# Second block: GLA score pieces as three fp32r products, and an earlier order for the gates and a later one for the MLA latents

## The chip, the cores and the metric

The kernel runs on one core of one Trainium2 chip. Times are device microseconds from launch to end. Three runs of the kernel before gave 2714.05, 2717.61 and 2721.09 us; their median, 2717.61, is what a forecast is compared with.

## The reference, cut to what matters

The program is two transformer-like blocks in a row, each with two layers, on 256 tokens of width 1024. All arithmetic is fp32. The change touches the second block's mixer alone, which runs once per layer:

```python
zin = h @ w_in
(cq, ckv, kpe, sg_uv, gq, gk, gv, g_lr, g_og, dq, dk, dv, da, db, dz, gates) = split(zin)
o_a = mla_branch(cq, ckv, kpe, ...)          # latents -> norm -> w_uq, w_ukv -> rope -> attention
o_b = spatial_gating_branch(sg_uv, ...)
o_c = gla_branch(gq, gk, gv, g_lr, g_og, ...)
o_d = deltanet_branch(dq, dk, dv, da, db, dz, ...)
```

The gated linear attention (GLA) computes, for 4 heads with keys of 32:

```python
log_a  = log_sigmoid(gate_lr @ w_gate + b_gate) / 16     # low-rank gates, per head and key element
cum    = cumsum(log_a)
scores = einsum('bhik,bhjk,bhijk->bhij', q, k, exp(cum_i - cum_j)) for i >= j
o      = scores @ v   (and the carried state; then norm and output gate)
```

## The kernel before, in words

**Matrix work.** The kernel keeps fp32 accuracy in its projections by splitting each operand into a high part, rounded to fp32r, and a low part, what is left, also held as fp32r. A product is then three fp32r products: low with high, high with low, high with high. ScalarE (ACT) makes the high part of the weights (`hi`), VectorE (DVE) the low part by a subtraction (`lo`). Smaller products inside the branches are plain fp32 matmuls. In the trace a plain fp32 matmul leaves two weight loads and two matmul records, an fp32r one leaves one of each, and so does a transpose.

**Parts.** The weights of one pass of the second block come in 84 parts of 128x2048 elements through a ring of three buffers. SyncE (SP) starts the load of part h once the low part of h-3 is made. Parts 0 and 1 are the MLA latents (`cq_fill`), part 2 a few narrow columns, among them the low-rank gates, parts 3 to 11 the other projections, parts 12 to 31 the gates and the branch products. `in_fill(h)` runs the 48 products of a part in two halves, m = 0 and m = 1, each of 8 steps k of three products with 256 columns streamed, which I call wide products.

**The order is written out by hand.** TensorE (PE) calls `between(h, m, k)` after each step, `mid(h)` between the halves and `after(h)` at the end of part h; there the small products of the branches are put. ACT and DVE run loops over i, where `hi(i + 2)` and `lo(i + 1)` alternate with what belongs to the branches. Semaphores hold the rest: `pe.wait_ge(sem, n)` stands in PE's queue, and everything behind it waits too.

**GLA scores.** The lower triangle of the 256x256 scores is put together from 9 levels j: one for the block of the second half of the tokens against the first (j = 0), seven for halves within ever smaller squares, and one (j = 4) with the raw q and k for the diagonal. For each level q and k are scaled by exp of a difference of cumulated logs (`level_diffs`, `level_exps`, `level_inputs`), four levels at a time: qeA, keA and then qeB, keB. A level has 8 pieces (4 heads, 2 blocks of 128 tokens; level 0 has 4), each a product over the 32 rows of a head, 128 columns loaded and 128 streamed. `gla_piece(j, p)` runs one piece per step of parts 13 to 17. DVE takes each level out of PSUM by a masked copy (`scores`), and two levels' PSUM banks alternate, so level j waits for the copy of j-2. `gla_out` multiplies the scores with v.

**What else the change moves.** `c_turn` transposes the MLA latents, `mla_up` projects them up, `rope_turn` does the rotation's half turn, `few_turn` does gate_lr @ w_gate and the transposes of the narrow columns, `softplus_1` to `_3` make the log gates, `cumulate` and `cumulated` their cumulative sums, `squared_norms` the deltanet's key norms, `decay_rows`, `kv_turn`, `lower_rows` and `key_products` belong to the deltanet's triangular system. The rows of `mem`, needed for cross attention, are loaded to `xm`, which shares its place with `probs`.

Of the kernel before, what the change touches and what calls it, by code (L numbers as in the profile page):

```python
# [7 lines left out]
F32 = mybir.dt.float32  # L8
# [8 lines left out]
P = 128  # L17
SEQ = 256
# [1286 lines left out]
def second_block(nc, ps, x, con, bfc, a):  # L1305
    with ExitStack() as ctx:
# [40 lines left out]
        qeB, keB = at("qeB", [P, 4, SEQ], offset=base), at("keB", [P, 4, SEQ], offset=base + 4096)  # L1347
        gates = at("gates", [P, 2, KD, SEQ], offset=base + 8192)
# [14 lines left out]
        qeA, keA = at("qeA", [P, 4, SEQ], offset=base), at("keA", [P, 4, SEQ], offset=base + 4096)  # L1363
        l2s, l2r = at("l2s", [P, 4, SEQ], offset=base + 8192), at("l2r", [P, 4, SEQ], offset=base + 12288)
# [10 lines left out]

        probs = at("probs", [P, 8, SEQ])
        xm = probs[:, :, :].rearrange("p (t a) b -> p t (a b)", t=NT)
# [5 lines left out]
        spb = at("spb", [P, 5, 264], offset=base)  # L1383


        base = place[0]
        dnp = at("dnp", [P, 6, SEQ + 4])
        rv, kd = at("rv", [P, NT, W2], offset=base), at("kd", [P, W2], offset=base + 2048)
# [38 lines left out]
        cum_ps, df_ok, le_ok, lev_ok = sem("cum_ps"), sem("df_ok"), sem("le_ok"), sem("lev_ok")  # L1427
        sa_zero, gp_ps, sa_ok, go_ps, go_ok, sil_ok, gn_ok = (
# [86 lines left out]
        def level(j):  # L1515


            if j == 4:
                return gqk[:, 0, :], gqk[:, 1, :]
            n = j if j < 4 else j - 1  # L1520
            return (qeA[:, n, :], keA[:, n, :]) if n < 4 else (qeB[:, n - 4, :], keB[:, n - 4, :])
# [60 lines left out]
        with nc.Fori(0, DEPTH) as l:  # L1582
            with nc.Block() as block:

                @block.sync
                def _(sp_):
# [35 lines left out]
                    for h, (_, _, source) in enumerate(parts):  # L1622
# [12 lines left out]
                        if h == 17:  # L1635

                            sp_.wait_ge(pt_ps, 1)
# [4 lines left out]
                def _(pe):  # L1642
# [135 lines left out]
                    def few_turn():  # L1778
                        pe.wait_ge(*freed[unit["in", FEW2]])
                        for t in range(NT):  # L1780
                            T.matmul(ps[:, 3, t * P:(t + 1) * P], fewS[:, t * P:(t + 1) * P], wg[:, :],
                                     start=True, stop=True)
                        for t in range(NT):
                            mm = T.transpose(ps[:, 3, SEQ + t * P:SEQ + (t + 1) * P], fewS[:, t * P:(t + 1) * P], ident)
# [1251 lines left out]
```

## Time and profile before

| | |
|---|---|
| median of three runs | 2717.61 us (2714.05 to 2721.09) |
| the profiled execution | 2721.69 us, its span 2719.9 us, mean granted TensorE clock 0.935 |
| PE busy | 2527.3 us, 93% of the span |
| DVE busy, ACT busy | 1424.9 us (52%), 1092.8 us (40%) |
| DMA | 370.35 MB, mean 136 GB/s |

The first block takes the time to about 1261 us, then come the second block's two passes, from 1291 us and from 2000 us. The profile's line PEclk gives the TensorE clock granted in each of 40 slices of 68 us, in tenths of full speed. The clock has two levels, 2.4 GHz (1.00) and 1.2 GHz (0.50). "PE" rows are matmuls, whose ends are modelled, "PEld" rows are weight loads. A timeline row gives the start, the length from the first start to the last end, and how many records are merged in it; x2 is one plain fp32 piece. For how long PE is held, the distance from start to start tells more than the lengths, since records overlap.

### The profile page before, as it was taken

To read this page: it belongs to the slowest core of one execution; us is meant where nothing else is said; L and a number is where in the kernel's file an instruction comes from. 1 tells how busy PE (TensorE), PEld (TensorE's weight loads), DVE (VectorE), ACT (ScalarE), POOL (GpSimd) and SP (SyncE) were. 2 spreads that over 40 slices of the span, in tenths; PEclk is the share of its full clock that TensorE was granted. 3 is DMA by queue.
4 is the path that set the end of the run, shared out by engine and by line. 5 is a ranking of instruction groups with operands and counts; after the bars stand their busy time and mean duration, and the time that the engine had idled before them with its cause. 6 is when DMAs were issued, how large, how long until landed. Compare 5 with 4: busy or idle time off the path is not lost. (4 is left out here: it accounts for less than half of the span.)

```text
span 2719.9 us, 40921 instructions
## 1 busy us (share of the span) xinstructions
PE 2527.3 (93%) x17400; PEld 2316.2 (85%) x17400; DVE 1424.9 (52%) x1539; ACT 1092.8 (40%) x1356; POOL 48.4 (2%) x49
## 2 busy tenths in 40 slices
PE   6999998996999998995899999989959999998996
PEld 6988998986988998994787898989859789898985
DVE  6555465455555456453653467445537245754453
ACT  3533544343534444342451324444425213344342
POOL 0000000000000000000000000000000000000000
PEclk9999999998999999997895899999979669999998
DMA  6423455544533354551641234445444213354552
GB/s 200 152 83 113 133 187 167 180 180 116 181 94 94 122 189 155 186 187 55 184 131 31 78 99 150 155 143 183 170 133 128 71 47 94 109 171 155 163 194 85
DMA packets 300003, 370.35 MB, mean 136 GB/s; under 512 B 25006, under 2 KB 267300, under 8 KB 299812
## 3 DMA queue, kind: packets, MB, share of 16 engines
q1 hardware_dynamic: 299812, 367.62, 42.8%
q8 instruction: 142, 2.33, 0.4%
q14 instruction: 49, 0.40, 0.0%
HBM read 366.55 MB, written 1.05 MB: 135 GB/s over the span
## 5 line engine op out<-in xcount | busy, mean ns | idle before, releaser
L398 PE MATMUL ps<-a_nhi,a_wlo 128*128 128x256 f32 x1792 | 524.8, 293 | 12.0 <-DVE a_nlo L951 10.4
L398 PE MATMUL ps<-a_nlo,a_whi 128*128 128x256 f32 x1792 | 507.9, 283 | 0.0
L398 PE MATMUL ps<-a_nhi,a_whi 128*128 128x256 f32 x1792 | 507.6, 283 | 0.0
L921 DVE TENSOR_TENSOR a_wlo<-a_ring,a_whi 128x2048 fp32r<-128x2048 f32 x174 | 395.5, 2285 | 107.9 <-ACT a_whi L705 107.4
L2430 DVE TENSOR_TENSOR b_wlo<-b_ring,b_whi 128x2048 fp32r<-128x2048 f32 (+1 forms) x168 | 379.2, 2261 | 134.9 <-ACT b_whi L2168 134.7
L1669 PE MATMUL ps<-b_nhi,b_wlo 128*128 128x256 f32 x1296 | 414.5, 320 | 19.3 <-ACT b_cqk L2186 11.8
L705 ACT CAST a_whi<-a_ring 128x2048 fp32r<-128x2048 f32 x174 | 331.1, 1905 | 194.9 <-PE ps L398 73.2
L2168 ACT CAST b_whi<-b_ring 128x2048 fp32r<-128x2048 f32 (+1 forms) x168 | 316.1, 1884 | 175.3 <-PE ps L2151 77.4
L1669 PE MATMUL ps<-b_nlo,b_whi 128*128 128x256 f32 x1296 | 386.2, 298 | 0.0
L1669 PE MATMUL ps<-b_nhi,b_whi 128*128 128x256 f32 x1296 | 385.8, 298 | 0.0
L398 PEld LDWEIGHTS ps<-a_nhi,a_wlo 128*128 128x128 f32 x1792 | 345.1, 193 | 18.1 <-DVE a_wlo L921 11.4
L398 PEld LDWEIGHTS ps<-a_nlo,a_whi 128*128 128x128 f32 x1792 | 344.8, 192 | 2.5 <-issue 2.4
L398 PEld LDWEIGHTS ps<-a_nhi,a_whi 128*128 128x128 f32 x1792 | 344.3, 192 | 0.0
L1669 PEld LDWEIGHTS ps<-b_nhi,b_wlo 128*128 128x128 f32 x1296 | 264.1, 204 | 51.1 <-issue 44.9
L1669 PEld LDWEIGHTS ps<-b_nlo,b_whi 128*128 128x128 f32 x1296 | 269.4, 208 | 0.1
L1669 PEld LDWEIGHTS ps<-b_nhi,b_whi 128*128 128x128 f32 x1296 | 268.7, 207 | 0.0
L2196 ACT ACTIVATE b_gates<-ps 128x512 f32<-128x512 f32 x32 | 19.1, 597 | 224.6 <-PE ps L1669 224.6
L2151 PE MATMUL ps<-b_whi,b_hlo 128*128 128x512 f32 x256 | 99.6, 389 | 0.0
L2151 PE MATMUL ps<-b_wlo,b_hhi 128*128 128x512 f32 x256 | 99.6, 389 | 0.0
L2151 PE MATMUL ps<-b_whi,b_hhi 128*128 128x512 f32 x256 | 99.6, 389 | 0.0
L2605 DVE COPY_PREDICATED b_SaT<-b_con,ps 128x1024 f32<-128x1024 uint32 x16 | 21.0, 1311 | 141.3 <-PE ps L1865 141.3
L1242 DVE TENSOR_TENSOR a_gates<-a_ffg,ps 128x512 f32<-128x512 f32 x22 | 15.1, 688 | 142.5 <-PE ps L398 142.5
(531 smaller groups left out, 4604.5 us busy)
## 6 DMA issues: line engine op xcount, KB each, us to landing
a_ring<-in_w_in SPq DMA_DIRECT2D x50, 1024.0 KB, 5.3
b_ring<-in_w_in SPq DMA_DIRECT2D x50, 1024.0 KB, 6.1
a_ring<-in_w_ffn_in SPq DMA_DIRECT2D x44, 1024.0 KB, 5.3
a_ring<-in_w_gate SPq DMA_DIRECT2D x32, 1024.0 KB, 5.3
b_ring<-in_w_up SPq DMA_DIRECT2D x32, 1024.0 KB, 5.6
b_ring<-in_w_down SPq DMA_DIRECT2D x32, 1024.0 KB, 4.9
a_ring<-in_w_ffn_out SPq DMA_DIRECT2D x22, 1024.0 KB, 5.0
a_ring<-in_w_branch SPq DMA_DIRECT2D x16, 1024.0 KB, 5.1
```

What stands on the lines that cost most here:

```text
L398: mm = T.matmul(out, w[:, k, c:c + P], x_[:, k, :], start=k == 0 and n == 0, stop=k == KD - 1 and n == 2)
L705: S.copy(part(whi, h), part(ring, h)).then_inc(hi_ok, 1)
L921: V.tensor_tensor(part(wlo, h), part(ring, h), part(whi, h).bitcast(F32), ALU.subtract).then_inc(lo_ok, 1)
L1242: V.tensor_tensor(hid[:, 2 * c:2 * c + 2, :], ffg[:, c % 2, :].rearrange("p (b c) -> p b c", b=2), ps[:, 4 + c % 2, :].rearrange("p (b c) ...
L1669: mm = T.matmul(out, w[:, k, c:c + P], x_[:, k, :], start=k == 0 and n == 0, stop=k == KD - 1 and n == 2)
L2151: mm = T.matmul(ps[:, 4 + 2 * t + half, :], hidden_of(x_, i)[:, kk, t * P:(t + 1) * P], w[:, kk, half * 512:(half + 1) * 512], start=i + k ...
L2168: A.copy(part(whi, h), part(ring, h)).then_inc(hi_ok, 1)
L2196: ins = A.activation(gates[:, g // 4 % 2, 2 * (g % 4):2 * (g % 4) + 2, :], b.rearrange("p (a b) -> p a b", a=2), gate_func)
L2430: V.tensor_tensor(part(wlo, h), part(ring, h), part(whi, h).bitcast(F32), ALU.subtract).then_inc(lo_ok, 1)
L2605: V.copy_predicated(SaT[:, :, :, :], m, level_out(j)).then_inc(sa_ok, 1)
```

## The change

GLA pieces: the scaled q and k of each group of levels, and the raw ones, get a high part on ACT (`level_hi`, and a copy to qkh) and a low part on DVE (`level_lo`, `raw_lo`). A piece is then three fp32r products. Pieces start half a part later. PE's order of the small products changes: few_turn goes to after part 3 and to PSUM bank 7, c_turn to after part 4, mla_up to after part 5, rope_turn to after part 6, cumulate from after part 9 to after part 7, gla_out into the middle of part 18, kv_turn into the middle of part 19. ACT's and DVE's orders follow, and some waits name other semaphores.

```diff
@@ sync
-                        if h == 17:
-                            sp_.wait_ge(pt_ps, 1)
+                        if h == 21:
+                            sp_.wait_ge(gp_ps, pieces_to(4))
                             sp_.dma_start(xm[:, :, :], a["mem_2"]...).then_inc(mem_in, 16)
@@ tensor: mla_up, few_turn
                         pe.wait_ge(ct_ok, 1)
-                        pe.wait_ge(w_in_, 48)
+                        pe.wait_ge(spv, 1)
...
                         pe.wait_ge(*freed[unit["in", FEW2]])
+                        pe.wait_ge(w_in_, 48)
@@ squared_norms / cumulate / spatial_mix
-                        pe.wait_ge(spv, 1)
+                        pe.wait_ge(eg_in, 1)
-                        pe.wait_ge(l2_rt, 1)
+                        pe.wait_ge(ct_ok, 1)
-                        pe.wait_ge(eg_in, 1)
+                        pe.wait_ge(l2_rt, 1)
@@ gla_piece
                             if j == 0:
-                                pe.wait_ge(lev_ok, 1)
+                                pe.wait_ge(ll_ok, 1)
+                            if j == 4:
+                                pe.wait_ge(qkl_ok, 1)
                             if j == 5:
-                                pe.wait_ge(lev_ok, 2)
+                                pe.wait_ge(ll_ok, 2)
...
-                        q_, k_ = level(j)
+                        q_hi, q_lo, k_hi, k_lo = level(j)
                         r = slice(32 * h, 32 * h + 32)
                         tq_ = 1 if j == 0 else t
-                        T.matmul(level_out(j)[:, h, t, :], k_[r, t * P:(t + 1) * P], q_[r, tq_ * P:(tq_ + 1) * P],
-                                 start=True, stop=True).then_inc(gp_ps, 1)
+                        for n, (k_, q_) in enumerate(((k_lo, q_hi), (k_hi, q_lo), (k_hi, q_hi))):
+                            mm = T.matmul(level_out(j)[:, h, t, :], k_[r, t * P:(t + 1) * P], q_[r, tq_ * P:(tq_ + 1) * P],
+                                          start=n == 0, stop=n == 2)
+                        mm.then_inc(gp_ps, 1)
@@ between / mid / after
-                        if 13 <= h <= 17 and 2 * (h - 13) + m < 9:
-                            gla_piece(2 * (h - 13) + m, k)
+                        if 13 <= h <= 17 and 2 * (h - 13) + m > 0:
+                            gla_piece(2 * (h - 13) + m - 1, k)
...
                         if h == 18:
+                            gla_out()
                             decay_rows()
+                        if h == 19:
+                            kv_turn()
...
                         if h == 3:
+                            few_turn()
+                        if h == 4:
                             c_turn()
-                        if h == 4:
+                        if h == 5:
                             mla_up()
-                            few_turn()
-                        if h == 5:
+                        if h == 6:
                             rope_turn()
+                        if h == 7:
+                            cumulate()
                         if h == 8:
                             squared_norms()
-                        if h == 9:
-                            cumulate()
...
-                        if h == 17:
-                            gla_out()
-                        if h == 18:
-                            kv_turn()
@@ scalar
+                    def level_hi(g, qe_, ke_, qh_, kh_):
+                        act.wait_ge(lev_ok, g + 1)
+                        A.copy(qh_[:, :, :], qe_[:, :, :])
+                        A.copy(kh_[:, :, :], ke_[:, :, :]).then_inc(lh_ok, 1)
...   (latents' eviction from i == 4 to 5, mla_up's from 5 to 6, gate exps 6 to 5, Ln 7 to 6,
...    level_exps(0) 11 to 10, level_exps(1) 14 to 13, squares of mem 20 to 22)
+                        if i == 12:
+                            level_hi(0, qeA, keA, qhA, khA)
+                            A.copy(qkh[:, :, :], gqk[:, :, :]).then_inc(qkh_ok, 1)
...
                         if i == 14:
                             turn_hi(0)
-                            level_exps(1, keB)
+                            act.wait_ge(o_ps, 1)
+                            level_hi(1, qeB, keB, qhB, khB)
@@ vector
+                    def level_lo(g, qe_, ke_, qh_, kh_, ql_, kl_):
+                        dve.wait_ge(lh_ok, g + 1)
+                        V.tensor_tensor(ql_[:, :, :], qe_[:, :, :], qh_[:, :, :].bitcast(F32), ALU.subtract)
+                        V.tensor_tensor(kl_[:, :, :], ke_[:, :, :], kh_[:, :, :].bitcast(F32), ALU.subtract
+                                        ).then_inc(ll_ok, 1)
+
+                    def raw_lo():
+                        dve.wait_ge(qkh_ok, 1)
+                        V.tensor_tensor(qkl[:, :, :], gqk[:, :, :], qkh[:, :, :].bitcast(F32), ALU.subtract
+                                        ).then_inc(qkl_ok, 1)
...   (softplus_1 from i == 5 to 4, _2 from 6 to 5, _3 from 7 to 6; cumulated and level_diffs(0) to 8;
...    level_inputs(0) and level_diffs(1) to 11; level_lo(0) at 12; raw_lo and level_inputs(1) at 13;
...    level_lo(1) at 14; scores(j), turn_lo, gate_gain half a part to one part later;
...    gla_result and lower_rows ahead of lo(20); norm_in(2) from 22 to 23)
```

## Rows read from the trace of the kernel before

**Rows 1.** The page: PE's busy time, and the granted clock in 40 slices.
```profile
PE 2527.3 (93%) x17400; PEld 2316.2 (85%) x17400; DVE 1424.9 (52%) x1539; ACT 1092.8 (40%) x1356; POOL 48.4 (2%) x49
...
PEclk9999999998999999997895899999979669999998
```

**Rows 2.** Windows: length, busy time per engine, granted clock, DMA share, GB/s.
```profile
1318.00:1404.00 86.00, 86.00 (x649) 80.13 (x650) 61.26 (x87) 48.52 (x67) 4.54 (x3) 0.97 0.52 142
1404.40:1417.90 13.50, 13.50 (x76) 10.31 (x75) 4.07 (x8) 4.22 (x6) 0.00 (x0) 1.00 0.41 148
1417.90:1513.40 95.50, 95.39 (x295) 70.64 (x296) 30.85 (x21) 12.76 (x13) 0.00 (x0) 0.50 0.16 44
...
2124.40:2226.80 102.40, 102.29 (x320) 76.18 (x320) 31.81 (x21) 14.12 (x14) 0.00 (x0) 0.50 0.15 41
...
1531.70:1540.60 8.90, 8.90 (x55) 7.04 (x53) 0.00 (x0) 2.33 (x2) 0.00 (x0) 1.00 0.41 118
```

**Rows 3.** Windows, of line L1865 alone: PE and PEld busy, records, clock.
```profile
1404.40:1417.90 13.50, 6.28 (x26) 3.80 (x26) 1.00 0.41 148
1417.90:1513.40 95.50, 43.56 (x110) 27.36 (x110) 0.50 0.16 44
2113.90:2124.40 10.50, 4.75 (x20) 2.91 (x20) 1.00 0.50 189
2124.40:2226.80 102.40, 46.00 (x117) 28.85 (x116) 0.50 0.15 41
```

**Rows 4.** Timelines of PE and PEld, pieces at full clock (start, us).
```profile
1404.41 0.48 PE L1865 MATMUL ps<-b_qeA,b_keA 32*128 32x128 f32 x2
1404.82 0.39 PE L1669 MATMUL ps<-b_nhi,b_wlo 128*128 128x256 f32 x1
...
1405.16 0.28 PE L1669 MATMUL ps<-b_nhi,b_whi 128*128 128x256 f32 x1
1405.37 0.48 PE L1865 MATMUL ps<-b_qeA,b_keA 32*128 32x128 f32 x2
...
1404.82 0.19 PEld L1669 LDWEIGHTS ps<-b_nhi,b_wlo 128*128 128x128 f32 x1
1404.93 0.19 PEld L1669 LDWEIGHTS ps<-b_nlo,b_whi 128*128 128x128 f32 x1
```

**Rows 5.** The same at half clock.
```profile
1426.99 0.79 PE L1865 MATMUL ps<-b_qeA,b_keA 32*128 32x128 f32 x2
1427.71 0.58 PE L1669 MATMUL ps<-b_nhi,b_wlo 128*128 128x256 f32 x1
...
1428.65 0.58 PE L1865 MATMUL ps<-b_qeA,b_keA 32*128 32x128 f32 x1
...
1427.71 0.29 PEld L1669 LDWEIGHTS ps<-b_nhi,b_wlo 128*128 128x128 f32 x1 [0.22 <-issue]
1427.88 0.33 PEld L1669 LDWEIGHTS ps<-b_nlo,b_whi 128*128 128x128 f32 x1
```

**Rows 6.** Timeline of PE in the first block: fp32r products after bf16 ones.
```profile
107.60 0.31 PE L478 MATMUL ps<-a_cumS,a_sel 128*128 128x128 f32 x1
107.75 0.23 PE L479 MATMUL ps<-bfc 128*128 128x128 bf16 x1
107.78 0.36 PE L398 MATMUL ps<-a_nhi,a_wlo 128*128 128x256 f32 x1
107.99 0.28 PE L398 MATMUL ps<-a_nlo,a_whi 128*128 128x256 f32 x1
```

**Rows 7.** Timeline of PE: products with 64 columns streamed.
```profile
1396.62 2.79 PE L1835 MATMUL ps<-b_mv,b_pT 128*128 128x64 f32 x24
```

**Rows 8.** All waits of PE from 1318 to 1542 us.
```profile
PE ps L1669 <- ACT b_cqk L2186: 6.4, 1, 6.4
```

**Rows 9.** Timelines of DVE and PE around part 9.
```profile
1365.82 2.28 DVE L2430 TENSOR_TENSOR b_wlo<-b_ring,b_whi 128x2048 fp32r<-128x2048 f32 x1
...
1368.45 1.89 PE L1798 MATMUL ps<-b_l2s,b_con 128*128 128x256 f32 x8
```

More of the change, by code:

```diff
@@ L1373, in second_block @@
         hhi, hlo = (at(n, [P, SPLITS, 2 * SEQ], F32R, offset=base + i * 6144) for i, n in enumerate(("hhi", "hlo")))
+        base = place[0]
         probs = at("probs", [P, 8, SEQ])
+        qhA, khA = at("qhA", [P, 4, SEQ], F32R, offset=base), at("khA", [P, 4, SEQ], F32R, offset=base + 4096)
         xm = probs[:, :, :].rearrange("p (t a) b -> p t (a b)", t=NT)
@@ L1518, in level @@
             if j == 4:
-                return gqk[:, 0, :], gqk[:, 1, :]
+                return qkh[:, 0, :], qkl[:, 0, :], qkh[:, 1, :], qkl[:, 1, :]
             n = j if j < 4 else j - 1
-            return (qeA[:, n, :], keA[:, n, :]) if n < 4 else (qeB[:, n - 4, :], keB[:, n - 4, :])
+            return tuple(b[:, n % 4, :] for b in ((qhA, qlA, khA, klA) if n < 4 else (qhB, qlB, khB, klB)))
         def pieces_to(j):
@@ L1779, in few_turn @@
                         pe.wait_ge(*freed[unit["in", FEW2]])
+                        pe.wait_ge(w_in_, 48)
                         for t in range(NT):
-                            T.matmul(ps[:, 3, t * P:(t + 1) * P], fewS[:, t * P:(t + 1) * P], wg[:, :],
+                            T.matmul(ps[:, 7, t * P:(t + 1) * P], fewS[:, t * P:(t + 1) * P], wg[:, :],
                                      start=True, stop=True)
                         for t in range(NT):
-                            mm = T.transpose(ps[:, 3, SEQ + t * P:SEQ + (t + 1) * P], fewS[:, t * P:(t + 1) * P], ident)
+                            mm = T.transpose(ps[:, 7, SEQ + t * P:SEQ + (t + 1) * P], fewS[:, t * P:(t + 1) * P], ident)
                         mm.then_inc(pre_ps, 1)
@@ L2301, in _ @@
                         hi(i + 2)
-                        if i == 4:
+                        if i == 5:
                             act.wait_ge(ct_ps, 1)
@@ L2307, in _ @@
                             ins.then_inc(ct_ok, 1)
-                        if i == 5:
+                        if i == 6:
                             act.wait_ge(up_q, 1)
@@ L2331, in _ @@
                             exps(1)
+                            level_exps(0, keA)
                         if i == 11:
@@ L2490, in softplus_1 @@
                         v3 = spb[:, 0, :].rearrange("p (t c) -> p t c", t=NT)
-                        pre, few = (ps[:, 3, i * SEQ:(i + 1) * SEQ].rearrange("p (t c) -> p t c", t=NT) for i in range(2))
+                        pre, few = (ps[:, 7, i * SEQ:(i + 1) * SEQ].rearrange("p (t c) -> p t c", t=NT) for i in range(2))
                         V.scalar_tensor_tensor(v3[:, :, 0:P], pre, -1.0, bg[:, :].unsqueeze(1).broadcast_to([P, NT, P]),
@@ L2783, in _ @@
                             maxima(1)
-                            cumulated()
                         if i == 11:
@@ L2787, in _ @@
                             V.tensor_copy(pT[:, 4:8, :], L[:, 4:8, :]).then_inc(pt_v, 1)
-                        if i == 18:
+                        if i == 19:
                             gla_result()
                             head_norm_1(4)
+                            lower_rows()
                         if i == 20:
@@ L2803, in _ @@
                             mla_norms()
+                        if i == 4:
+                            softplus_1()
                         if 4 <= i <= 6:
@@ L2807, in _ @@
                         if i == 5:
-                            softplus_1()
+                            softplus_2()
                         if i == 6:
-                            softplus_2()
+                            softplus_3()
                         if i == 7:
                             rope()
-                            softplus_3()
                         if i == 8:
+                            cumulated()
+                            level_diffs(0, keA)
                             layer_norm_1()
@@ L2860, in _ @@
                             if i < 26:
-                                if i == 22:
+                                if i == 23:
                                     norm_in(2, 5, xm)
```

47 lines of the change are left out of this document (27 added, 20 removed).

## The prediction

> **What bounds the kernel now.** The page first, for the engines' shares and for where the clock is low: TensorE (PE) is busy 93% of the span, and the clock line has, beside short dips, two long ones, slices 22 and 23 and slices 32 and 33 of 40, one in each pass of the second block [rows 1]. Then the windows, for these dips: from 1417.9 to 1513.4 us and from 2124.4 to 2226.8 us the granted clock is 0.50, the lower of its two levels (1.2 GHz), while PE is busy throughout. Ahead of each, and from 1531.7 us, it is 1.00 (2.4 GHz) [rows 2]. Then one source line in these windows: the score pieces of the gated linear attention (GLA), L1865. Each piece leaves two matmul records, so the dips hold 227 records, 113.5 pieces, and 46 records, 23 pieces, run at full clock ahead of them [rows 3]. Last the waits, to see whether PE ever stood still around the rest of the change: between 1318 and 1542 us it has one wait, 6.4 us for b_cqk, ahead of everything that is moved [rows 8]. So the stretch is bound by PE's own queue. What an edit adds or takes in that queue shows in the time one for one, and what it does on DVE and ACT costs nothing as long as their results come before PE asks for them.
>
> **One piece, as it is.** A step of the projection is three wide fp32r products, then a piece. At full clock a step takes 1405.37 - 1404.41 = 0.96 us. The piece starts 1405.37 - 1405.16 = 0.21 after the last wide product; 256 columns at 2.4 GHz are 0.107 of it, so some 0.1 passes until the array is drained. From the piece's start to the next wide product are 0.41 us. There the first wide load starts 0.11 before the second, so a load that can't hide takes 0.107 to 0.11 [rows 4]. 0.41 less load and drain leaves 0.2 for the two records, 0.1 each: a plain fp32 record with 128 columns holds the array like 256 columns, 0.107, and its second load hid behind the first record's stream. At half clock a step takes 1428.65 - 1426.99 = 1.66 us. Piece to wide product is 0.72, an unhidden load 0.165 (1427.71 to 1427.88) [rows 5]; with two streams of 0.213 (256 columns at 1.2 GHz) 0.13 is left for the drain. So a step costs 0.70 us more in the dips than at full clock.
>
> **The three products.** Each piece becomes three fp32r products of 32 rows, 128 columns loaded, 128 streamed. Drain and the change to and from 32 rows stay as they are, once each. The trace has no such product, but the first block has an fp32r one with 128 columns streamed: after a bf16 product it takes 107.75 - 107.60 = 0.15 us, and one with 256 columns in the same position takes 107.99 - 107.78 = 0.21 [rows 6]. The difference, 0.06 for 128 columns, says one pass over the columns, 0.066 with the little extra that fp32r shows. So the streams are short, and the loads between them bound the piece. At full clock: 24 records with only 64 columns streamed take 2.79 us, under 0.12 each [rows 7], so successive loads come 0.11 apart. The inside of the new piece is 0.107 + 0.11 + 0.11 + 0.066 = 0.39 where it was 0.107 + 2 x 0.107 = 0.32: 0.07 more, times 23 pieces is +1.6 us.
> At half clock no row shows loads closer than 0.213 apart, since streams cover them. Bounds for their spacing: 0.107, as at full clock (the load then has nothing to do with the array's clock), and 0.213, twice that (it goes wholly with the clock). Inside of the piece before: 0.165 + 2 x 0.213 = 0.59. After, with spacing s: 0.165 + 2s + 0.107. With 0.107 that is 0.49, 0.105 less; with 0.213 it is 0.70, 0.107 more. The nearest row is the load that can't hide in the same dip, 0.165 [rows 5]; with it the inside is 0.60, 0.01 more. I take that: 113.5 x 0.01 = +1.2 us. The ends are -11.9 and +12.1 us.
>
> The Trainium skill, TensorE: Matmul & The Clock Gate, "What overlaps and what doesn't", has a rule against this change: a weight load overlaps with running matmuls only where its row group differs, and the three products of a piece lie in one row group. The trace disagrees for the piece as it is: without overlap the 0.41 us of [rows 4] would be 0.107 x 4 + 0.09 = 0.52. What the rule would cost here is a rival below.
>
> **Does the clock stay low?** Before each fall PE had just gone from pieces on every second step to pieces on each step, with no idle time, and the clock stayed at 1.2 GHz until the pieces ended. The new step has the same three wide products and a narrow part that also has 32 rows, with 3 x 128 columns streamed in place of two records that each hold the array twice as long. Nothing in it gives the array more to do, so I keep both dips, and they still hold 8 of the 9 sets of pieces. The whole block of pieces starts half a part later and ends half a part later (part 13's first half is now plain, part 17's second is not), which moves the dips and doesn't lengthen them; the gate changes in jumps, so a few us either way are in the range.
>
> **Splits on ACT and DVE.** ACT gets two sets of two 128x1024 copies and one 128x512 copy, DVE two sets of two 128x1024 subtractions and one of 128x512, per pass of the block. By DVE's 2.28 us for 128x2048 elements [rows 9], and the same on ACT, that is some 5 us each. They lie in 1390 to 1440 us. In the dip DVE is busy 31 us of 95.5 and ACT 13; in 1318 to 1404 us DVE is busy 61 of 86 us and ACT 49 [rows 2]. Hidden, cost 0. The first set is due at part 13's second half, some 3 us later than pieces start today; DVE has it done about when part 13 starts. Without that cover its wait would be up to 2.5 us per pass, the two subtractions.
>
> **Moved steps.** The gate turns (six records and transposes), the latent turn, the up-projection, the rope turn and the cumulative sums go to other places in PE's queue, with the same instructions: sum 0 if nothing is late. The parameters they need are asked for 14 us sooner, but no DMA is moved past another, and PE's only wait there is the one named. The longest DVE chain moves in part: softplus's last step goes before the rope, the cumulative sums and first level differences go ahead of the layer norm. Tightest is part 9. Today DVE's low part for it runs 1365.82 to 1368.10 and PE's norms start at 1368.45 with eight records, 1.5 us, part 9 behind them [rows 9]. After, cumulate (twelve records, some 1.5 us) stands before part 8 and leaves its old place after part 9, so the norms start at about 1369.9. They now also wait for the cumulated copies, four small ones and one of 128x256, which follow that low part and take about 1 us: due at 1369.1. So slack is some 0.8 us, cost 0; behind the norms stand part 9 and all of PE's queue. gla_out and kv_turn move from the ends of parts 17 and 18 into the middles of 18 and 19, with their records unchanged; the last masked copy (128x1024, some 1.2 us) has half a part, 24 wide products or 2.9 us, to be done, where today it had the same. lower_rows goes before part 20's low half, and the key products that wait for it come later than it by about 3 us. The load of the memory rows moves later in SP's queue, from part 17 to part 21; SP would hold all following weight loads there if its wait on the pieces were open, but those pieces end some 30 us sooner. Its squares on ACT, two of 128x1024, go to part 22, where ACT has time while PE works at half a part ahead of the solve's products: 0.
>
> **Sum.** +1.6 + 1.2 = +2.8 us on the profiled execution's own 2721.69 us (span 2719.9), so 2724.5. That execution lies 4.1 us above the median of the runs, 2717.61, and the forecast for a median is 2717.61 + 2.8 = 2720.4, no change that can be told: this kernel's measurement tells about 0.3%, 8.2 us.
>
> **Rivals.**
> (a) Slower: at half clock loads follow each other at 0.213. Mechanism: in the dips the load goes wholly with the array's clock, so three loads cost more than two long streams; it decides from a spacing of 0.165 up by 0.21 us per piece for each 0.1 us. For it: the streams double exactly there. Against it: the load that can't hide takes 0.165, not 0.213 [rows 5]. Sum 1.6 + 12.1 = +13.7, 2731.
> (b) Slower: loads don't hide in a piece. Full clock: 3 x (0.107 + 0.066) = 0.52 for 0.32, +0.20 x 23 = 4.6. Half: 3 x (0.165 + 0.107) = 0.82 for 0.59, +0.225 x 113.5 = 25.5. Together +30, 2748. Against it [rows 4], as worked out above. This is the skill's rule as named there.
> (c) Faster: the load keeps 0.107 at half clock. 1.6 - 11.9 = -10.3, 2707. For it: at full clock the load's 0.107 and the stream's 0.053 per 128 columns differ by two, as if it had a clock of its own. Against it: 0.165.
> The Trainium skill, same page, "LDWEIGHTS (loading the stationary operand)", gives the load's time by its columns over 1.2 and names no dependence on the array's clock; that is this rival.
> (d) Faster: the clock doesn't fall, or falls late and returns early. All steps at 0.96: 113.5 x (1.66 - 0.96) = 79 us less, and 136.5 x 0.07 = 9.6 more: -70, 2648. For it: in 1531.7 to 1540.6 us narrow products stand in each step too (64 rows, four records), and the clock stays at 1.00 [rows 2]. Against it: the new piece streams less than the old one under which the clock fell.
> (e) A new wait: the norms of part 9 behind the cumulated copies, or the first level's low parts behind their highs. Each us of lateness is paid twice; 3 us late gives 2720.4 + 6 = 2726.
>
> **Chances.** Forecast 0.40, (a) 0.22, (b) 0.05, (c) 0.15, (d) 0.12, (e) 0.06. The forecast and (e) are within 0.3% (I give (e) a third of slower), (a) and (b) slower, (d) faster, and (c), just over the bound, two parts faster to one the same: faster 0.22, same 0.49, slower 0.29. The likeliest case's own range is 2714 to 2727. The range asked for takes in both bounds of the load and the gate's jumps: 2704 to 2737. It leaves out (d), (b).
>
> **What would show it.** The dips at about the same length in the clock line. L1865 (its successor) with three records per piece; PE starts inside it 0.11 apart at full clock and 0.165 at half, with 0.107 or 0.213 for (c) or (a). Steps of 1.03 and 1.67 us. No PE wait from 1318 to 1542 us but that for b_cqk. The forecast is wrong if the clock is 1.00 where pieces stand on each step, if the step at half clock is off 1.67 by 0.07 or more, or if a wait of over 2 us is in that stretch.

## The result and the profile after

The kernel after takes 2738.75 us (median of 6 executions, 2734.56 to 2739.55), the kernel before, on the same chip, 2721.3 (2714.05 to 2727.31): ratio 1.0061, 95% interval [1.0043, 1.0079]. The forecast was 2720.4, with a range of 2704 to 2737. The change costs some 17 us, a small rise (0.6%) but clear of the noise, and the time lies 1.75 us beyond the range. Two disturbed executions, one of the kernel before at 7995.27 us (beside e0) and one of e5 at 4077.2 us, stand in no ratio and in no spread given below. The profiled execution has a span of 2736.7 us, where before had 2719.9.

The page of the kernel after, PE's busy time and its clock line, answers to [rows 1]: 136 matmuls more, and the two long dips as before.

```profile
PE 2545.1 (93%) x17536; PEld 2347.5 (86%) x17536; DVE 1434.9 (52%) x1549; ACT 1100.9 (40%) x1366; POOL 44.2 (2%) x49
...
PEclk9999999998999999997995899999979659999998
```

Windows of the kernel after (columns as in [rows 2]): the steps with pieces ahead of each dip, then the dip.

```profile
1411.10:1428.40 17.30, 17.30 (x108) 14.24 (x108) 8.09 (x7) 8.14 (x8) 0.00 (x0) 1.00 0.34 101
1428.40:1527.40 99.00, 99.00 (x347) 81.13 (x347) 28.77 (x19) 10.23 (x10) 0.00 (x0) 0.50 0.18 53
2125.20:2135.00 9.80, 9.80 (x63) 8.12 (x62) 5.25 (x4) 5.73 (x6) 0.00 (x0) 1.00 0.25 80
2135.00:2244.20 109.20, 109.20 (x378) 88.96 (x379) 31.62 (x21) 12.71 (x13) 0.00 (x0) 0.50 0.20 57
```

The dips are 99.0 and 109.2 us long where they were 95.5 and 102.4. Of their length, how much is pieces? The same windows for the piece's line alone, three records to a piece now, answer to [rows 3].

```profile
1411.10:1428.40 17.30, 8.29 (x46) 6.19 (x47) 1.00 0.34 101
1428.40:1527.40 99.00, 47.36 (x159) 37.41 (x159) 0.50 0.18 53
2125.20:2135.00 9.80, 4.49 (x25) 3.37 (x26) 1.00 0.25 80
2135.00:2244.20 109.20, 53.72 (x180) 42.45 (x180) 0.50 0.20 57
```

(159 + 180) / 3 = 113 pieces lie in the dips, as before (113.5). So what is longer is the piece. Timelines of PE and of the weight loads, one step at half clock, against [rows 5]:

```profile
1470.35 0.58 PE L1676 MATMUL ps<-b_nhi,b_wlo 128*128 128x256 f32 x1
...
1471.29 0.47 PE L1876 MATMUL ps<-b_qhB,b_klB 32*128 32x128 f32 x1
1471.56 0.41 PE L1876 MATMUL ps<-b_qlB,b_khB 32*128 32x128 f32 x1
1471.77 0.41 PE L1876 MATMUL ps<-b_qhB,b_khB 32*128 32x128 f32 x1
1472.12 0.58 PE L1676 MATMUL ps<-b_nhi,b_wlo 128*128 128x256 f32 x1
...
1471.28 0.28 PEld L1876 LDWEIGHTS ps<-b_qhB,b_klB 32*128 32x128 f32 x1 [0.22 <-issue]
1471.45 0.33 PEld L1876 LDWEIGHTS ps<-b_qlB,b_khB 32*128 32x128 f32 x1
1471.67 0.33 PEld L1876 LDWEIGHTS ps<-b_qhB,b_khB 32*128 32x128 f32 x1
```

A step takes 1472.12 - 1470.35 = 1.77 us (forecast 1.67, before 1.66). Inside the piece the second load follows the first by 0.17, but the third follows the second by 0.22, and the last two products start 0.21 apart. So the load that meets a drained array takes 0.17 here, and one behind another load comes 0.21 after it. At full clock (the same view):

```profile
1413.84 0.33 PE L1876 MATMUL ps<-b_qhA,b_klA 32*128 32x128 f32 x1
1414.01 0.27 PE L1876 MATMUL ps<-b_qlA,b_khA 32*128 32x128 f32 x1
1414.12 0.27 PE L1876 MATMUL ps<-b_qhA,b_khA 32*128 32x128 f32 x1
1414.32 0.39 PE L1676 MATMUL ps<-b_nhi,b_wlo 128*128 128x256 f32 x1
...
1414.87 0.33 PE L1876 MATMUL ps<-b_qhA,b_klA 32*128 32x128 f32 x1
```

A step is 1414.87 - 1413.84 = 1.03, as forecast. The waits of PE from 1318 to 1550 us answer to [rows 8]: still only that for b_cqk.

```profile
PE ps L1676 <- ACT b_cqk L2198: 7.0, 1, 7.0
```

**Where the time lies.** Every PE record of parts 13 to 19 was put down to the function that issues it, each by the distance from its start to the next record's start. The table is worked out from the records of the traces. It gives both passes added, in us; the rows from e1 on belong to the experiments below.

```
kernel                      pieces   all else    sum
before                        91.6      184.9   276.5
before, second profile        87.2      179.3   266.5
after                        104.4      184.7   289.1
after, second profile        106.0      187.4   293.4
e1  one plain product         89.7      183.0   272.7
e2  two fp32r products        75.0      178.4   253.4
e10 one fp32r product         48.1      170.3   218.4
e5  plain, pairs, same rows   44.9      124.2   169.1
e6  plain, pairs, other rows  31.2      124.1   155.3
e4  plain, bursts of four     22.3      123.6   145.9
e7  plain, bursts of eight    25.1      118.3   143.4
e8  e4 in after's order       22.9      128.1   151.0
e3  three, bursts of four     29.3      127.9   157.2
e9  plain, all 128 rows       26.3      124.1   150.4
```

From before to after the pieces take 12.9 us more (before rounding) and all else 0.3 less. By steps: 113 x 0.107 + 23 x 0.06 = 13.5.

The time at which the clock falls differs from pass to pass, so passes are best compared where it falls alike. With an early fall, parts 13 to 19 take 139.7 us in the kernel before (second pass of both profiles, falls 10.6 and 10.8 us after the first piece) and 146.7 in the kernel after (second pass of the first profile, both passes of the second, falls at 9.7, 10.2 and 11.2 us). The first pass of e1, which has the order of after with plain pieces, takes 139.7 with a fall at 10.6. So at an equal fall the new pieces cost 7.0 us in each pass, 14.0 in both, and the moved steps and the splits cost nothing there.

Of the 16.8 us between the two spans another 3.1 lie ahead of the second pass of the first block (659.65 us against 656.54 in before), whose code is the same in both; in the second profile of the kernel after that stretch ends at 657.72. Some of it is there at the first matmul, which comes at 15.2 us in before, 17.0 in after and also 17.0 in e4, a kernel in the old order. So this part is not the change's. The time outside of parts 13 to 19 (span less sum) is 2443.4 and 2443.2 us in the two profiles of before, 2447.6 and 2445.4 in those of after; the other kernels in the old order have 2442.2 to 2446.9, those in the new order 2443.1 to 2446.2. No cost of the moves can be told in it.

### The profile page after: what moved, and what is told of

It reads as the page before. It is cut to its first block and busy times, and to the rows that moved or that the text cites. A ratio compares the mean times of both kernels' runs of the same rounds, so it can differ in the third digit from the quotient of the medians.

```text
span 2736.7 us, 41233 instructions
## 1 busy us (share of the span) xinstructions
PE 2545.1 (93%) x17536; PEld 2347.5 (86%) x17536; DVE 1434.9 (52%) x1549; ACT 1100.9 (40%) x1366; POOL 44.2 (2%) x49
## 5 line engine op out<-in xcount | busy, mean ns | idle before, releaser
L398 PE MATMUL ps<-a_nhi,a_wlo 128*128 128x256 f32 x1792 | 526.8, 294 | 10.9 <-DVE a_nlo L951 9.3
L398 PEld LDWEIGHTS ps<-a_nhi,a_wlo 128*128 128x128 f32 x1792 | 347.0, 194 | 17.4 <-DVE a_wlo L921 10.7
L773 ACT ACTIVATE a_probs<-ps,a_nmx 128x128 f32<-128x128 f32 (+1 forms) x96 | 39.2, 429 | 94.5 <-DVE a_nmx L1072 94.5
```

Source lines behind the costliest of these rows:

```text
L398: mm = T.matmul(out, w[:, k, c:c + P], x_[:, k, :], start=k == 0 and n == 0, stop=k == KD - 1 and n == 2)
L773: ins = S.activation(probs[:, s, 0:w], L[:, s, 0:w], ACT.Exp, bias=nmx[:, n % 2, s:s + 1], accum_out=rsum[:, n % 2, s:s + 1])
```

## Experiments

Ratios are to the kernel before, run beside each on the same chip.

**e1: one plain product in the new order.**

```diff
-for n, (k_, q_) in enumerate(((k_lo, q_hi), (k_hi, q_lo), (k_hi, q_hi))):
-    mm = T.matmul(out, k_[...], q_[...], start=n == 0, stop=n == 2)
+mm = T.matmul(out, k_hi.bitcast(F32)[...], q_hi.bitcast(F32)[...], start=True, stop=True)
```

> The kernel after, with each piece as one plain fp32 product of the high parts (two records) in place of the three fp32r products; the low parts are left out of the scores. Order, splits and waits are those of the kernel after. Theory A (the whole loss is in the pieces: 0.107 us more for each at half clock, 0.06 at full, some 13 us): same time as before, ratio 1.000 within 0.0015, steps of 0.96 and 1.66 us, dips of some 95 and 102 us. Rival B (the moved steps, the splits or something ahead of the second block cost the 4 to 5 us that the pieces don't explain): ratio 1.0015 to 1.002, and the second block's first product still some 3 us later than before.

2719.26 us, ratio 1.0016 [0.9994, 1.0037]. Most of the loss goes with the three products, although splits, waits and moves are all there: the interval ends below that of the change, [1.0043, 1.0079]. The ratio itself lies at the point between both theories, 1.0015, and doesn't decide between them (the kernel before against itself, e11 below, gives 1.0018). The profile does: at an equal fall of the clock a pass takes 139.7 us, as in before. Rival B's other sign, a second block that starts 3 us late, is no sign of the order either: its first matmul comes at 1299.72 us here, at 1297.69 and 1297.19 in the two profiles of before, and at 1300.75 in e4, which has the old order. The windows of its two dips (columns as above) say more: 102.4 and 85.4 us.

```profile
1420.20:1522.60 102.40, 102.29 (x320) 76.19 (x320) 31.63 (x21) 12.71 (x13) 0.00 (x0) 0.50 0.21 60
2143.80:2229.20 85.40, 85.34 (x270) 64.02 (x269) 24.31 (x16) 8.95 (x9) 0.00 (x0) 0.50 0.21 62
```

One kernel, two passes of the same code, and the second dip is 17 us shorter: there the clock fell 21.5 us after the first piece, in the first pass 10.6.

**e11: the kernel before once more.**

> The kernel before once more, for a second profile of it. Its executions lie between 2700 and 2727 us, with a mean clock of 0.944 to 0.933 that goes with them; those of the kernel after between 2734 and 2741. Theory A: what differs between executions is when the clock falls after the first piece (13.5 and 10.5 us after it in the first profile, up to 21 in a variant), 0.7 us for each step that still runs at full clock; everything outside of parts 13 to 19 keeps its length within 3 us in all. A fall 7 us later would take 5 us off. Rival: the executions differ elsewhere (first block, transfers), the stretches of the pieces are 137 and 140 us again.

2722.55 us against 2712.82 for the other executions of the same kernel, ratio 1.0018 [0.9994, 1.0042]; together they reach from 2702.58 to 2725.95. In the profile (windows ahead of and in the dips) the first fall comes 27.3 us after the first piece instead of 13.5, the second after 10.8 as before.

```profile
1404.50:1431.80 27.30, 27.30 (x150) 20.59 (x149) 8.48 (x11) 9.10 (x10) 0.00 (x0) 1.00 0.33 112
1431.80:1503.50 71.70, 71.59 (x223) 53.15 (x223) 26.32 (x17) 7.85 (x8) 0.00 (x0) 0.50 0.16 44
2103.70:2114.50 10.80, 10.80 (x62) 8.37 (x62) 3.13 (x7) 2.87 (x4) 0.00 (x0) 1.00 0.49 185
2114.50:2216.90 102.40, 102.29 (x321) 76.23 (x321) 31.81 (x21) 14.11 (x14) 0.00 (x0) 0.50 0.15 41
```

Theory A holds: parts 13 to 19 of the first pass take 126.7 us for 136.8, and those of the second 139.7 in both profiles; outside of them the two profiles differ by 0.2 us. The time of this kernel hangs on when the clock falls. The other executions bear it out. For 63 of them the span and the mean granted clock are on record, and 2 x (1 - clock) x span estimates the time at half clock. The spans rise by 0.38 us with each us of it (correlation 0.96), from 2697.7 us at a clock of 0.944 to 2725.4 at 0.933.

**e0: the kernel after once more.**

> The kernel after once more, beside the kernel before on this chip. Theory A (13 us in the pieces at half clock, the rest is where the clock happens to fall in each execution): median 2729 to 2736 with a spread of some 10 us or more over the runs, ratio 1.005 to 1.007, and the second block's first product not later than before by 3 us in every execution. Rival B (4 to 5 us more are lost for good in the moved steps): ratio 1.0065 or over, spread of 5 us.

2739.55 us (2735.1 to 2740.89), ratio 1.0072 [1.005, 1.0093]. The spread is 6 us, not 10 or more, and the median and the ratio lie above theory A's: both signs named for rival B came. Yet what it says, 4 to 5 us lost in the moved steps, isn't in the profile: both passes take 146.7 us, no more than the early pass of the first profile, and in e1 the moved steps cost nothing. What is left is early falls. Both come early here, 10.2 and 11.2 us after the first piece, with dips of 109.2 us each, and the stretch of the pieces is 293.4 us.

```profile
1419.50:1528.70 109.20, 109.20 (x379) 89.02 (x380) 31.63 (x21) 12.71 (x13) 0.00 (x0) 0.50 0.19 57
2139.70:2248.90 109.20, 109.20 (x381) 89.38 (x382) 31.63 (x21) 12.71 (x13) 0.00 (x0) 0.50 0.19 54
```

**e2 and e10: two fp32r products, and one.**

```diff
-enumerate(((k_lo, q_hi), (k_hi, q_lo), (k_hi, q_hi)))
+enumerate(((k_hi, q_lo), (k_hi, q_hi)))                  # e2
+T.matmul(out, k_hi[...], q_hi[...], start=True, stop=True)   # e10
```

> The kernel after with two fp32r products for each piece, low part of k times high part of q left out. Theory A (a product more is a load more, 0.213 us apart at half clock and 0.11 at full): 0.213 x 114 + 0.11 x 22 = 27 us less than the kernel after, so some 2711, 10 us under before (ratio 0.996), step at half clock 1.55 us. Rival C (the piece has a fixed part, and a product costs its stream of 0.107 at half clock): 12 + 1 = 13 us less than after, 2725, step 1.66.

> The kernel after with one fp32r product for each piece, high parts only. With three the piece takes 0.829 us to the next wide product at half clock, with two 0.616. Theory A (a fixed 0.34 for the change back, and each further product a load of 0.213, the first of them 0.275): 0.34, so 0.38 under the plain piece of before: 113.5 x 0.38 + 23 x 0.2 = 48 us less than before (0.982) with the dips there. Rival C: the changes of rows stay and less work lies between them, so the clock falls as soon or sooner: a few us more than that. Rival D: the clock stays at 1.00, 120 us less.

e2: 2705.93, ratio 0.9969 [0.9948, 0.999]; e10: 2668.72 (2645.93 to 2675.58), 0.9805 [0.9732, 0.9879]. Timelines of PE at half clock, first e2, then e10:

```profile
1450.53 0.58 PE L1676 MATMUL ps<-b_nhi,b_wlo 128*128 128x256 f32 x1
...
1451.47 0.47 PE L1876 MATMUL ps<-b_qkl,b_qkh 32*128 32x128 f32 x1
1451.74 0.41 PE L1876 MATMUL ps<-b_qkh 32*128 32x128 f32 x1
1452.09 0.58 PE L1676 MATMUL ps<-b_nhi,b_wlo 128*128 128x256 f32 x1
```

```profile
1449.88 0.58 PE L1676 MATMUL ps<-b_nhi,b_wlo 128*128 128x256 f32 x1
...
1450.82 0.47 PE L1875 MATMUL ps<-b_qhB,b_khB 32*128 32x128 f32 x1
1451.22 0.58 PE L1676 MATMUL ps<-b_nhi,b_wlo 128*128 128x256 f32 x1
```

From the piece's start to the next wide product: 0.40 us with one product, 0.62 with two, 0.83 with three (1472.12 - 1471.29). So each further product is 0.21, theory A of e2, and 0.34 expected for one alone was 0.06 too little. The prediction's own terms give all three: 0.165 for the load on the drained array, 0.107 for one pass over the columns and 0.13 for the drain are 0.40, and each 0.213 of spacing more makes it 0.615 and 0.83. If the columns took two passes, one product alone would be 0.51; so it is the loads that stand 0.213 apart. The plain piece of before, 0.72, lies between two and three. In e10 the clock fell 33.7 and 18.1 us after the first piece, later than with three (9.7 to 17.4), against its rival C. Its total near the 0.982 expected is in part luck: against the first profile of before the pieces take some 43 us less and all else 15 less, where the expectation had 48 in the pieces and the dips as they were.

**e3 and e4: bursts of four.** e3 is made from the kernel after, e4 from the kernel before. The edit of e4 (that of e3 is the same, with after's `> 0` and `- 1` in the conditions):

```diff
-if 13 <= h <= 17 and 2 * (h - 13) + m < 9:
-    gla_piece(2 * (h - 13) + m, k)
+if 13 <= h <= 17 and 2 * (h - 13) + m < 9 and k in (1, 5):
+    for p in range(k - 1, k + 3):
+        gla_piece(2 * (h - 13) + m, p)
```

> The kernel after, with the pieces of a level in two bursts of four (behind the wide products 1 and 5 of a half) instead of one behind each of eight. Theory A (what makes a piece dear is the change between 128 and 32 rows: at half clock 0.345 us into it for 0.213 and 0.341 out of it): a burst of twelve products takes 0.275 + 10 x 0.213 + 0.341 = 2.75 us where four pieces took 4 x 0.829 = 3.32, and three changes ahead of it at 0.132 go too: 0.97 us less for a burst at half clock, 0.7 at full: with 28 and 6 bursts, 31 us less than after, 2708 (ratio to before 0.995), the dips still there. Rival B (each change of the row group inside a burst drains the array too): only the 0.132 goes, 0.4 for a burst, 13 us less, 2726. Rival C: the array does more in the same time and the clock stays at 1.00: a further 60 to 70 us less, 2640 to 2650.

> The kernel before, with its plain fp32 pieces in two bursts of four for each level. Theory A (the change of rows is what costs): eight records take 0.375 + 6 x 0.213 + 0.345 = 2.0 us at half clock where four pieces took 2.88, and 3 x 0.132 goes: 1.28 us less for a burst, some 0.8 at full clock: 27 and 7 bursts, 40 us less than before, 2681 (0.985). Rival B (a drain at each change of row group): 0.4 for a burst, 12 us less, 2709 (0.9955). Rival C: the clock stays at 1.00, a further 60 to 70 us less.

e3: 2604.31 (2602.47 to 2607.58), ratio 0.9596 [0.9569, 0.9623]. e4: 2594.58 (2592.99 to 2595.4), 0.9556 [0.9526, 0.9586]. Rival C on top of A, for both, and more than C had it: it gave 2640 to 2650 for e3 and, by the same sum, 2611 to 2621 for e4. In e3 the clock still falls near the end of each stretch of pieces, for 6.8 us in the first pass and 3.4 in the second, with 12 and 8 of the pieces' 408 records in them. The windows of e4 over its two stretches of pieces show the clock at 1.00 from the first piece to the last. First e3's first stretch, then e4's two:

```profile
1407.30:1454.50 47.20, 44.39 (x417) 40.38 (x416) 35.29 (x24) 15.67 (x16) 0.00 (x0) 0.97 0.37 102
1407.80:1450.10 42.30, 40.03 (x347) 35.08 (x348) 31.17 (x26) 16.60 (x18) 0.00 (x0) 1.00 0.37 115
2053.40:2095.80 42.40, 40.13 (x349) 35.19 (x348) 31.27 (x26) 16.61 (x18) 0.00 (x0) 1.00 0.37 116
```

And a burst is shorter than theory A had it. Timeline of PE in e4, eight records between two wide products:

```profile
1421.13 0.28 PE L1669 MATMUL ps<-b_nhi,b_whi 128*128 128x256 f32 x1
1421.34 0.71 PE L1865 MATMUL ps<-b_qeA,b_keA 32*128 32x128 f32 x8
1421.98 0.38 PE L1669 MATMUL ps<-b_nhi,b_wlo 128*128 128x256 f32 x1
```

0.64 us for four pieces, where one by one at full clock each takes 0.41 [rows 4]. The next two experiments say why.

**e5 and e6: pairs.** The kernel before with two pieces behind every second step (of three wide products); in e5 the list is ordered so that the two are on the same 32 rows (and two waits on the pieces follow the new order, not shown); in e6 it is as it was, the two on rows 0 to 31 and 64 to 95, or 32 to 63 and 96 to 127.

```diff
-if 13 <= h <= 17 and 2 * (h - 13) + m < 9:
-    gla_piece(2 * (h - 13) + m, k)
+if 13 <= h <= 17 and 2 * (h - 13) + m < 9 and k % 2:
+    for p in range(k - 1, k + 1):
+        gla_piece(2 * (h - 13) + m, p)
 # e5 only
-PIECES = [(0, 0), (2, 0), (0, 1), (2, 1), (1, 0), (3, 0), (1, 1), (3, 1)]
+PIECES = [(0, 0), (0, 1), (2, 0), (2, 1), (1, 0), (1, 1), (3, 0), (3, 1)]
```

> The kernel before, its pieces in pairs behind every second wide product, both of a pair on the same 32 rows (the two halves of one head). A piece pair can't run side by side, so only changes of rows go: one of two. At half clock a pair then takes 0.375 + 2 x 0.213 + 0.345 = 1.15 us for 1.44, and 0.132 goes ahead of it: 0.43 less for each of 57 pairs, 0.3 for 11 at full clock: theory A 28 us less than before with the dips as they are (ratio 0.99). Theory C (the share of the array's time that is work decides over the clock): the array does more in a step, the clock falls later or not at all, up to 80 us less.

> The kernel before, pieces in pairs behind every second wide product, the two of a pair on rows 0 to 31 and 64 to 95. In the burst of four such neighbours started 7 ns apart, so a pair costs what one piece costs: 0.72 + 0.13 less at half clock, 0.41 + 0.09 at full. Theory A (dips as they are): 57 x 0.85 + 11 x 0.5 = 54 us less than before (0.98). Theory C: the clock stays at 1.00 or nearly: 110 to 120 us less than before (0.957 to 0.96). Rival D: the pair on other rows is no cheaper than the pair on the same rows: equal to e5.

e5: 2615.23, ratio 0.9618 [0.9585, 0.9651], 107 us less than the kernel before beside it: the 28 of theory A and the 80 that theory C had at most. e6: 2600.13, 0.9565 [0.9537, 0.9592], 122 us less, where theory C had 110 to 120. PE's timeline of e5, then of e6:

```profile
1420.99 0.71 PE L1865 MATMUL ps<-b_qeA,b_keA 32*128 32x128 f32 x4
1421.63 0.66 PE L1886 MATMUL ps<-con,b_ob 128*128 128x128 f32 x4
```

```profile
1420.65 0.49 PE L1865 MATMUL ps<-b_qeA,b_keA 32*128 32x128 f32 x4
1421.07 0.39 PE L1669 MATMUL ps<-b_nhi,b_wlo 128*128 128x256 f32 x1
```

Four records on the same rows take 0.64 us, four on two groups of rows 0.42, as long as one piece alone. (In e5 a 128-row transpose follows here; the median of its 64 pairs is 0.64 as well.) So pieces on different rows do run side by side, loads included; e4's eight records take what e5's four take. But most of the gain doesn't need this. In e5 nothing runs side by side, and its clock stays at 1.00 as well, in both passes; the first:

```profile
1404.90:1459.60 54.70, 54.42 (x354) 45.37 (x354) 32.43 (x26) 16.62 (x18) 0.00 (x0) 1.00 0.31 95
```

The Trainium skill, TensorE: Matmul & The Clock Gate, "Why this matters for your kernels", says that products of few rows run concurrently when each has another group of rows. These traces agree (four records in 0.42 us for 0.64), where no wide product stands between the two pieces.

**e9: all 128 rows.**

```diff
-r = slice(32 * h, 32 * h + 32)
+r = slice(0, P)
```

> The kernel before, each piece at its place, one plain product behind each wide one, but over all 128 rows in place of its head's 32 (the sum over four heads: the scores are not those of the reference). The same count of instructions and columns, no change of rows. Theory A (the change of rows is what costs): piece and next wide product start 0.11 to 0.12 apart, step at full clock 3 x 0.12 + 2 x 0.11 = 0.58 us for 0.96. If the clock then stays at 1.00: 113.5 x 1.08 + 23 x 0.38 = 131 us less, 2590 (0.952). If it falls as before: step 1.07, 76 us less, 2645 (0.972). Rival B (a plain record in each step is what costs, whatever its rows): no change.

The scores are then not those of the reference. 2594.63 us, ratio 0.9546 [0.9495, 0.9596]. First the window over its first stretch of pieces, then a timeline of PE:

```profile
1405.20:1452.00 46.80, 43.79 (x359) 43.07 (x358) 32.81 (x26) 17.14 (x18) 0.00 (x0) 0.96 0.37 112
...
1420.58 0.36 PE L1669 MATMUL ps<-b_nhi,b_wlo 128*128 128x256 f32 x1
...
1420.90 0.28 PE L1669 MATMUL ps<-b_nhi,b_whi 128*128 128x256 f32 x1
1421.02 0.39 PE L1865 MATMUL ps<-b_qeA,b_keA 128*128 128x128 f32 x2
1421.16 0.36 PE L1669 MATMUL ps<-b_nhi,b_wlo 128*128 128x256 f32 x1
```

With the same two records and no change of rows the piece takes 0.14 us for 0.41, and starts 0.12 after the wide product for 0.21. A step is 0.58 us (1421.16 - 1420.58), as theory A had it. The clock stays up but for one fall of 3.4 us, 41 us after the first piece of the first pass; in the second pass it doesn't fall. So the change between 128 and 32 rows, twice in each step, costs time itself, and it stands in the steps before the long falls. Whether it is what brings the clock down isn't shown: each kernel here that keeps its clock (e3 to e9) has fewer changes and also puts its products through the array in less time, and no run separates the two. e10 keeps the changes with less work between them, and there the clock falls later, not sooner.

**e8: the new order, without the dips.** The kernel after with one plain product for each piece (as in e1) and bursts of four (as in e3).

> The kernel after with one plain fp32 product of the high parts for each piece (low parts left out of the scores), in bursts of four: order, splits and waits of the kernel after, pieces of the bursts of the kernel before. With no long dip its times spread by 2 us only, so it weighs the moved steps. Theory A (they cost nothing): the time of the kernel before with bursts, 2594.6, within 2 us. Rival B (they cost the 4 to 5 us): 2599. The kernel after with bursts (2604.3) less this is then the price of the three products at full clock: 34 bursts x (0.82 - 0.64) = 6 us.

2597.63 us, ratio 0.9549 [0.9522, 0.9575] (e4: 2594.58, 0.9556). The time lies between the two theories and the ratios are equal, but the stretch of parts 13 to 19 is 151.0 us for 145.9. The window over its first stretch of pieces shows a clock of 0.96, and the second is alike: the clock falls for 3.4 us near the end of each, in e4 not at all.

```profile
1408.50:1453.50 45.00, 41.43 (x350) 36.51 (x348) 35.33 (x24) 15.75 (x16) 0.00 (x0) 0.96 0.38 104
```

Its waits of PE from 1404 to 1482 us:

```profile
PE ps L1875 <- DVE b_SaT L2640: 2.0, 1, 2.0
PE ps L1676 <- ACT b_gates L2208: 1.6, 2, 0.8
```

In e4 the wait for DVE's scores (b_SaT) is 0.3 us. The scores, moved later by the change, come late once PE is fast; that is 2 us in each pass. In the kernel after the slow pieces hide them, so the moves cost nothing there (all else 184.7 for 184.9). Over both passes PE's waits there are 7.2 us for 4.5 in e4, so 2.7 of the 5.1 us are waits; the rest is about what the two short falls cost, 6.8 us at half clock at 0.38 us each (e11), an estimate. So the moves are free beside the dips and not without them. e3 less e8 in the stretch is 6.2 us, as expected for three products at full clock.

**e7: bursts of eight.** As e4 with `k == 3` and `for p in range(8)`.

> The kernel before, all eight pieces of a level in one burst. Theory A (each change to 32 rows and back costs some 0.19 us at full clock): 18 bursts fewer, 3 to 4 us less than with bursts of four (2594.6). Rival B: the fifth and sixth piece now wait for the first four to leave the array, 0.2 us or more in each of 18 bursts, which takes the gain back: 2594 to 2598.

2588.98 us (2588.17 to 2589.5), ratio 0.9527 [0.9477, 0.9577], the fastest of all. That is 5.6 us under e4, which ran on another chip; in the profiles the stretch of parts 13 to 19 is 2.5 us shorter (143.4 for 145.9), a little less than theory A's 3 to 4, and the rest lies outside of it. PE's timeline:

```profile
1420.33 1.51 PE L1865 MATMUL ps<-b_qeA,b_keA 32*128 32x128 f32 x16
1421.77 0.38 PE L1669 MATMUL ps<-b_nhi,b_wlo 128*128 128x256 f32 x1
```

Sixteen records take 1.44 us, where two bursts of eight take 1.28. By the starts of the single records the fifth piece begins 0.32 us after the fourth, where others begin 0.11 apart: the wait for the first pieces, rival B's point, is there. So the pieces take 2.8 us more than in bursts of four, and all else 5.3 less.

## Why the prediction was wrong

- **What bounds the kernel**: right. The stretch is PE's own queue, and what the change adds there shows one for one.
- **One piece, full clock**: right. 0.07 more was forecast, 0.06 came; step 1.03.
- **Spacing of the loads at half clock**: this is the step that failed. It took 0.165 us, the load that follows a drained array [rows 5], for loads behind one another. Those are 0.21 apart, which e2, e10 and the kernel after show alike. The term was +1.2 us and is 113 x 0.107 = 12.1. Rival (a) had this mechanism and its price (+13.7; measured are 12.9 between the profiles and 14.0 at equal falls of the clock), and too small a chance, 0.22. The row was of the right operation in the wrong position: an isolated load has no other load ahead of it. The upper bound, 0.213, was in the text as twice the full-clock spacing of [rows 7], and those rows are the ones with load behind load.
- **Clock**: both dips stayed, with the same 113 pieces in the profile compared (111 to 117 begin in dips in the two profiles of after, 99 to 113 in those of before). Rival (d) did not come, nor (b), nor (c). The pieces ahead of the falls were misread in a small point: the first level's four stand on the steps 0, 1, 4 and 5, not on every second one.
- **Splits, moves, waits**: cost 0, right; no new wait, so (e) did not come. e8 shows the cover they need: without the slow pieces 2 us of wait in each pass.
- **The base and the range**: 2717.61 was the median of three executions. The same kernel gives 2699.52 to 2727.31 over all its undisturbed executions, because the clock falls 10 to 27 us after the first piece and each step at half clock costs 0.7 more. So 2721.3 + 13.5 = 2735 is what the corrected sum gives beside the executions of the result, and rival (a)'s 2731 lacked 4 of that. The remaining 4 us to 2738.75 fit earlier falls in the kernel after (10 to 17 us after the first piece in two profiles, spread 6 us). The granted clocks on record point the same way: by the estimate of e11 the kernel before spends 346 us at half clock (63 executions), the kernel after 376 (12). Of these 30 us the longer pieces in the dips are 12; the other 18 would be work that ran at full clock before, at 0.38 us each some 7 us. That and the 14.0 of the pieces is nearly the 21.8 us between the mean spans of these executions (2714.5 and 2736.2, from several chips). Why three products bring the fall earlier stays open. The miss of 18.4 us is then 10.9 of spacing, less 0.2 at full clock, 3.7 of base and 4 of falls. The range took "a few us either way" for the gate's jumps; 10 would have been right, and one profile can't show it.

The Trainium skill, TensorE: Matmul & The Clock Gate, "LDWEIGHTS (loading the stationary operand)", prices a load by its columns over 1.2, 0.107 us for 128. The trace agrees at full clock (0.11) and not at half clock (0.21).

## What to carry to other kernels

Price an operation by a row in which it stands in the same position, behind the same neighbour and at the same clock; where the nearest row is an isolated one, take both bounds seriously; here the dearer one came. A product on fewer rows between wide ones costs two changes of the array, here 0.36 us at full clock around 0.14 of work (0.41 + 0.21 in before, 0.14 + 0.12 in e9): gather such products, and put those on different rows next to each other. Where the clock is low through a long stretch, ask first what would keep it up: that and the fewer changes were worth 120 us here (e4), nine times what the change of the products moved.

## What was not expected of the hardware

- With a 32-row piece behind every three wide products the clock falls to 1.2 GHz although PE never waits; with the same pieces in pairs or bursts of the old order (e4 to e7) it stays at 2.4 GHz, and on 128 rows (e9) it falls once for 3.4 us.
- When it falls differs between executions of one kernel: 27.3 and 13.5 us after the first piece in the same pass, 10 us of the time.
- Weight loads behind one another come 0.11 us apart at full clock and 0.21 at half; one that meets a drained array takes 0.11 and 0.17.
- A single product of one pass on 32 rows takes 0.40 us to the next wide one at half clock, more than the 0.34 from the last of several.
